# The order of work inside the chunk loop of a decoder layer: state product, right sides and first mask

## The chip, the cores and the metric

The kernel runs on one core of one Trainium2 chip. The metric is the device time of one execution in microseconds; of several executions the median counts. The profile is that of one execution, which has a time of its own.

## The reference

One layer of a hybrid decoder over 16 learned meta tokens and 2048 real tokens, width 1024. The input is RMS-normalised and projected once; then two branches read it. Branch B is stick-breaking attention and is not touched here. Branch A is RWKV-7 time mixing with 16 heads of dimension 64, whose core is a delta-rule recurrence over the tokens:

```
sa    = einsum("bhvk,bhk->bhv", state, kk)
state = state * decay - sa * (kk * a) + v * k
y     = einsum("bhvk,bhk->bhv", state, r)
```

After it each head's output is centred, divided by its standard deviation, and given a gain and a bonus. Both branches are gated, projected, merged and projected once more; the result is normalised and added to the input.

## The kernel before

The kernel has four stages one behind another: projections (up to about 2026 us), attention, the chunk loop of branch A (2956.7 to 3642.8 us of the span), and a tail with the branch and output projections. Only the chunk loop matters here; its functions are `tensor`, `scalar`, `vector`, `gpsimd` and `sync` inside `rwkv_programs`.

The recurrence is worked off in chunks of 64 tokens, 33 of them (`NCH`), padding and meta tokens in the first. Eight pairs of heads (`PAIRS`) lie on the 128 partitions, 64 for each head of a pair. For each chunk the kernel makes:

- **scores** (`score_products`, L1519): 16 matmuls of keys with queries into two double banks, `even` and `odd`. ScalarE copies one block of each to `NT` (L1660, L1661). VectorE masks all of it into `scores` (`masked`, L1717, two instructions);
- **the inverse of a triangular matrix** of 64x64 by blocks in five levels (`LEVELS`, `LAST` = 5). For each level `NT` is multiplied with that level's mask `tri` into `off` (L1767). A level is a `product` (L1582) of `off` with T, which VectorE makes into `X` (L1741), and an `advance` (L1595, in the last level L1597), which ScalarE copies to T or, in the last level, to `TT` (L1686), and VectorE transposes (L1751). Each is done in two halves of four pairs. T before level 1 is `off[0]` transposed (L1735), and the same with the unit matrix added (`tt_init`, L1785). Products and advances use the banks `even` and `odd` again;
- **right sides** (`right_sides`, L1552), which need the state before the chunk: ScalarE copies it beside the values (L1668, L1669, `s_kept`); then the **updates** `u` (L1560) with `TT`, copied by ScalarE (L1697, L1698); then the **state's product** (`next_state`, L1507) into the bank `chain`, to which VectorE adds the old state (L1727, `S_sum`) and which GpSimd scales (`S`, L1767, `s_done`);
- **outputs**: `value_products` (L1535) and `state_outputs` (L1568) into `y_bank`, centred values squared by ScalarE (L1674), the `variance` (L1527, L1528), the square root (L1702), reciprocals on VectorE (L1722) and three operations of GpSimd.
- **turned keys** (`turn_keys`, L1543), copied by ScalarE to `KBt` (L1653), for the state's product.

Every engine walks through bodies n = 0 to 36 (`walk`), and what follows the inverse lags: body n makes scores and inverse of chunk n, right sides, state outputs and updates of n - 1, and state's product and value products of n - 2. Each engine executes in the order written. TensorE's order in a body is state's product of n - 2, scores of n, value products of n - 2, key turns of n, right sides of n - 1, and then per level: product, something `beside_product`, advance, something `beside_advance`. What lies beside: state outputs in levels 1 and 2, updates in 3 and 4, the variance in 5. Order between engines is by semaphores that count up; `reach(eng, name, count)` waits for one. The scores of chunk n wait for all copies out of both banks of the chunk before:

```
reach(pe, "x_out", 10 * n)
reach(pe, "t_out", 10 * n)
```

All five masks of a chunk are made by GpSimd, and count on `off_done`. In the bodies 1 to 3 ScalarE and VectorE also split weights and outputs for the tail into high and low parts (L1706 to L1758).

Of the kernel before, what the change touches and what calls it, by code (L numbers as in the profile page):

```python
# [13 lines left out]
P = 128  # L14
# [1367 lines left out]
def rwkv_programs(nc, sem, t, io, scratch, tail, r, opening, y_parts_sent):  # L1382

    with ExitStack() as ctx:
# [11 lines left out]
        names = """zeroed kbt_pe kbt_out st_pe nt_out st_out off_done tt_init t0_out x_pe x_out t_pe t_out tt_out  # L1396
# [101 lines left out]
        def tensor(pe):  # L1498
# [74 lines left out]
            def body(n, b, turn):  # L1573
                def product(lv, half):
                    reach(pe, "off_done", LAST * n + lv)
# [24 lines left out]
                def beside_product(lv):  # L1600
# [9 lines left out]
                    if lv == 5 and inside(n, 2, 1):  # L1610
                        variance(n - 2, n)

# [11 lines left out]
                if inside(n, 2) and n <= NCH:  # L1624
                    next_state(n - 2)
                if inside(n, 0):
                    score_products(n, turn)
                if inside(n, 2, 1):
                    value_products(n - 2)
                if inside(n, 0):  # L1630
                    turn_keys(n)
                if inside(n, 1):
                    right_sides(n - 1)
# [14 lines left out]
        def scalar(act):  # L1648
# [6 lines left out]
            def body(n, b, turn):  # L1655
                b1, b2 = (b + 2) % 3, (b + 1) % 3
                if inside(n, 0):
                    reach(act, "st_pe", n + 1)
                    reach(act, "off_done", LAST * n)
                    act.copy(NT[0:DH, :, :], even[0:DH, :, 0:C]).then_inc(s["nt_out"], 1)  # L1660
                    act.copy(NT[DH:P, :, :], odd[DH:P, :, 0:C]).then_inc(s["nt_out"], 1)  # L1661
                if inside(n, 1):
                    reach(act, "s_done", n - 1)
                    if n == 1:
                        act.wait_ge(s["zeroed"], 1)
                    reach(act, "y_pe", n - 4)
                    reach(act, "s_pe", n - 3)
                    act.copy(VU[b1][0:DH, :, 0, :], S[b1][0:DH, :, :]).then_inc(s["s_kept"], 1)  # L1668
                    act.copy(VU[b1][DH:P, :, 1, :], S[b1][DH:P, :, :]).then_inc(s["s_kept"], 1)  # L1669
                if inside(n, 2, 1):  # L1670
# [41 lines left out]
        def vector(dve):  # L1712
            def body(n, b, turn):
# [10 lines left out]
                if inside(n, 2) and n <= NCH:  # L1724
                    reach(dve, "s_pe", n - 1)
                    reach(dve, "s_done", n - 2)
                    dve.tensor_tensor(S_sum[:, :, :], chain[:, :, :], S[b2][:, :, :], ALU.add).then_inc(s["s_sum"], 1)  # L1727
                if inside(n, 4, 1):
                    inverse_std(n - 4, slice(HP, PAIRS))
                if inside(n, 0):  # L1730
                    masked(0, even)
                    masked(1, odd)
                    for half in range(2):
                        reach(dve, "off_done", LAST * n + 1)
                        dve.transpose(T2[:, half, 0, :, :].rearrange("p k c -> p (k c)"),  # L1735
                                      off[0][:, HP * half:HP * half + HP, :].rearrange("p k c -> p (k c)")).then_inc(s["t0_out"], 1)
                for lv in range(1, LAST + 1):
# [5 lines left out]
                    if lv in (3, 4) and inside(n, 3, 1):  # L1743
                        inverse_std(n - 3, slice(lv - 3, lv - 2))
                    if lv == LAST and inside(n, 3, 1):
# [19 lines left out]
        def gpsimd(pool):  # L1765
# [3 lines left out]
            def body(n, b, turn):  # L1769
# [5 lines left out]
                if inside(n, 0):  # L1775
                    reach(pool, "nt_out", 2 * n + 2)
                    for lv in range(1, LAST + 1):
                        reach(pool, "x_pe", 10 * (n - 1) + 2 * lv)
                        if lv == 1:
                            reach(pool, "t0_out", 2 * n)  # L1780
                        tt(off[lv - 1][:, :, :], NT[:, :, :], tri[:, lv - 1, :].unsqueeze(1).broadcast_to(grid), ALU.mult, "off_done")
                        if lv == 1:
                            reach(pool, "t_pe", 10 * n)
                            reach(pool, "off_done", LAST * n + 1)
                            pool.tensor_tensor(T2[:, :, 1, :, :], off[0][:, :, :].rearrange("p (a k) c -> p a k c", a=2),  # L1785
                                               eye[:, :].unsqueeze(1).unsqueeze(1).broadcast_to([P, 2, HP, C]),
                                               ALU.add).then_inc(s["tt_init"], 1)
# [25 lines left out]
        def settled(eng):  # L1813

            banks_free(eng)
            for name, count in (("off_done", LAST * NCH), ("tt_init", NCH), ("t0_out", 2 * NCH), ("var_pe", NCH - 1), ("s_done", NCH - 1),
# [552 lines left out]
```

## Time and profile before

| | us |
|---|---|
| median of 3 runs | 4181.08 (4180.16 to 4187.48) |
| the profiled execution | 4177.68 |
| its span, first to last instruction | 4175.9 |
| the chunk loop in it | 2956.7 to 3642.8 |

| engine | busy share of the span | busy us in the chunk from 3250.40 to 3270.15 |
|---|---|---|
| TensorE (PE) | 97% | 19.20 of 19.75 |
| weight loads (PEld) | 80% | 17.84 |
| VectorE (DVE) | 56% | 14.63 |
| ScalarE (ACT) | 41% | 12.13 |
| GpSimd (POOL) | 20% | 13.53 |

Ends of matmuls are modelled, and the end of one overlaps the start of the next; so the length of a group of matmuls is best read from its start to the start of the next group.

### The profile page before, as it was taken

To read this page: it belongs to the slowest core of one execution; us is meant where nothing else is said; L and a number is where in the kernel's file an instruction comes from. 1 tells how busy PE (TensorE), PEld (TensorE's weight loads), DVE (VectorE), ACT (ScalarE), POOL (GpSimd) and SP (SyncE) were. 2 spreads that over 40 slices of the span, in tenths; PEclk is the share of its full clock that TensorE was granted. 3 is DMA by queue.
4 is the path that set the end of the run, shared out by engine and by line. 5 is a ranking of instruction groups with operands and counts; after the bars stand their busy time and mean duration, and the time that the engine had idled before them with its cause. 6 is when DMAs were issued, how large, how long until landed. Compare 5 with 4: busy or idle time off the path is not lost. (4 is left out here: it accounts for less than half of the span.)

```text
span 4175.9 us, 88867 instructions
## 1 busy us (share of the span) xinstructions
PE 4030.3 (97%) x34728; PEld 3322.7 (80%) x34728; DVE 2327.7 (56%) x3166; ACT 1709.1 (41%) x3428; POOL 817.4 (20%) x658
## 2 busy tenths in 40 slices
PE   7999999998899999999799999999899999999999
PEld 6888998887688888888566666666789988888887
DVE  5444545434643444444578888888567777633222
ACT  4222322222322222222376767676556665521111
POOL 3101111110211001111000000000256666600222
PEclk9999999999899999999899999999999999999999
DMA  2343333334233443433543344443333333265653
GB/s 90 116 124 116 111 109 94 109 116 149 66 109 114 121 121 114 121 102 116 132 98 85 83 94 100 96 101 67 100 112 107 106 108 115 80 218 166 208 176 126
DMA packets 482562, 479.67 MB, mean 115 GB/s; under 512 B 256784, under 2 KB 366992, under 8 KB 476128
## 3 DMA queue, kind: packets, MB, share of 16 engines
q1 hardware_dynamic: 469360, 445.85, 38.4%
q10 hardware_dynamic: 11520, 25.17, 1.7%
q0 software_dynamic: 1392, 4.54, 0.5%
q8 instruction: 212, 3.47, 0.3%
q14 instruction: 78, 0.64, 0.1%
HBM read 305.51 MB, written 169.93 MB: 114 GB/s over the span
## 5 line engine op out<-in xcount | busy, mean ns | idle before, releaser
L1251 ACT ACTIVATE keep<-z 128x512 f32<-128x512 f32 (+4 forms) x704 | 374.5, 539 | 192.7 <-PE z L1195 190.5
L1289 DVE TENSOR_TENSOR_SCAN kept<-keep,kept 128x512 f32<-128x512 f32 (+2 forms) x448 | 404.1, 954 | 26.7 <-ACT keep L1251 19.9
L1261 ACT COPY w<-turned 128x512 f32<-128x512 f32 (+4 forms) x704 | 371.5, 557 | 94.7 <-PE turned L1205 94.1
L1205 PE MATMUL turned<-t_identity,kept 128*128 128x128 f32 (+1 forms) x2432 | 364.2, 275 | 2.3 <-DVE kept L1289 2.3
L1286 DVE TENSOR_TENSOR_SCAN kept<-keep,hidden 128x512 f32<-128x512 f32 (+3 forms) x256 | 275.9, 1116 | 149.6 <-ACT keep L1251 148.9
L1194 PE MATMUL z<-k_high,q_parts 128*128 128x512 f32 (+4 forms) x704 | 303.3, 431 | 36.9 <-ACT keep L1251 16.7
L1205 PEld LDWEIGHTS turned<-t_identity,kept 128*128 128x128 f32 (+1 forms) x2432 | 280.2, 135 | 65.4 <-issue 12.4
L1232 PE MATMUL acc<-w,dv 128*64 128x512 f32 (+3 forms) x1280 | 288.1, 537 | 0.0
L1195 PE MATMUL z<-k_low,q_parts 128*128 128x512 f32 (+4 forms) x704 | 252.6, 359 | 0.0
L1767 POOL TENSOR_TENSOR off<-NT,tri 128x512 f32<-128x512 f32 x165 | 205.9, 1275 | 139.7 <-ACT NT L1661 139.7
L1194 PEld LDWEIGHTS z<-k_high,q_parts 128*128 128x128 f32 x704 | 133.8, 190 | 98.1 <-issue 42.8
L1232 PEld LDWEIGHTS acc<-w,dv 128*64 128x64 f32 x1280 | 94.4, 137 | 134.2 <-issue 120.8
L1582 PE MATMUL even<-T,off 64*64 64x64 f32 x5280 | 194.9, 222 | 4.3 <-issue 2.1
L1582 PEld LDWEIGHTS even<-T,off 64*64 64x64 f32 x5280 | 174.9, 136 | 18.2 <-issue 3.5
L1311 POOL DMA_DIRECT2D dv_diag<-scr_v_edge x15 | 7.3, 487 | 838.2 <-DMA dv_diag<-scr_dv 838.2
L1751 DVE STREAM_TRANSPOSE T<-T 128x256 f32<-128x256 f32 x264 | 117.6, 445 | 87.8 <-ACT T L1686 85.0
L1686 ACT COPY T<-odd 128x256 f32<-128x256 f32 x264 | 98.3, 373 | 158.7 <-PE odd L1595 146.9
L1741 DVE TENSOR_TENSOR X<-even,eye 128x256 f32<-128x256 f32 x330 | 139.4, 422 | 41.0 <-PE even L1582 33.5
L2108 DVE TENSOR_TENSOR y_lo<-y_raw,y_hi 128x512 fp32r<-128x512 f32 x61 | 44.8, 734 | 205.2 <-ACT y_hi L2052 205.2
L1595 PE MATMUL odd<-X,T 64*64 64x64 f32 x4224 | 151.8, 220 | 2.2 <-issue 1.8
L794 DVE CAST w_hi0B<-w_raw0B 128x1024 fp32r<-128x1024 f32 x40 | 41.7, 1042 | 197.6 <-PE pp3B L340 69.3
L794 DVE CAST w_hi0A<-w_raw0A 128x1024 fp32r<-128x1024 f32 x40 | 32.6, 815 | 203.0 <-PE pp4A L340 76.4
(566 smaller groups left out, 10880.7 us busy)
## 6 DMA issues: line engine op xcount, KB each, us to landing
w_raw0A<-in_w_main SPq DMA_DIRECT2D x42, 512.0 KB, 3.8
w_raw0B<-in_w_main SPq DMA_DIRECT2D x42, 512.0 KB, 3.8
w_raw1A<-in_w_main SPq DMA_DIRECT2D x41, 512.0 KB, 3.9
w_raw1B<-in_w_main SPq DMA_DIRECT2D x41, 512.0 KB, 3.9
KB<-scr_kb SPq DMA_DIRECT2D x33, 512.0 KB, 5.2
AR<-scr_ar SPq DMA_DIRECT2D x33, 512.0 KB, 5.9
y_raw<-scr_y SPq DMA_DIRECT2D x64, 256.0 KB, 4.4
merge<-scr_merge SPq DMA_DIRECT2D x64, 256.0 KB, 5.8
```

Of the source, the lines that this page charges most:

```text
L1194: pe.matmul(out, queries, k_high[u][:, k0:k0 + size], start=True, stop=False)
L1195: pe.matmul(out, queries, k_low[u][:, k0:k0 + size], start=False, stop=True).then_inc(logits_done, 1)
L1205: mm = pe.transpose(turned[num % TB][0:size, P * r:P * r + P], kept[kept_in(g)][:, src:src + size], t["identity"][:, :])
L1232: mm = pe.matmul(out, lhs, rhs, start=start, stop=stop, skip_group_check=True)
L1251: act.activation(keep[num % KB][:, 0:size], z[num % ZB][:, 0:size], ACT.Sigmoid, scale=-DH ** -0.5).then_inc(keep_done, 1)
L1261: act.copy(w[num % WB][0:size, c0:512], turned[num % TB][0:size, c0:512]).then_inc(copied, 1)
L1286: dve.tensor_tensor_scan(dst, data, hidden[:, 512 - size:][:, ::-1], 1.0, ALU.mult, ALU.max).then_inc(scanned, 1)
L1289: dve.tensor_tensor_scan(dst, data, data, kept[kept_in(g)][:, end:end + 1], ALU.mult, ALU.bypass).then_inc(scanned, 1)
L1582: mm = pe.matmul(x_bank(half)[hs, k, :], off[lv - 1][hs, HP * half + k, :], T2[hs, half, 0, k, :], start=True, stop=True)
L1595: mm = pe.matmul(p_bank(half)[hs, 0, k, :], T2[hs, half, 1, k, :], X[hs, half, k, :], start=True, stop=True)
L1741: dve.tensor_tensor(X[:, half, :, :], x_bank(half), eye[:, :].unsqueeze(1).broadcast_to([P, HP, C]), ALU.add).then_inc(s["x_out"], 1)
L1767: pool.tensor_tensor(out, a, b, op).then_inc(s[name], 1)
```

## The change

Three things move. On TensorE the state's product of chunk n - 1 stands in body n beside the fifth level's product, ahead of the advance, where before it was first in body n + 1; VectorE's sum moves with it. Right sides stand directly behind the scores; ScalarE makes its two copies of the state ahead of the two NT copies. And the first of the five masks is made by VectorE instead of GpSimd, between its two masked scores, with a semaphore of its own (`off_first`), on which the transposes and `tt_init` wait; `off_done` counts the other four.

```diff
@@ tensor
                 def product(lv, half):
-                    reach(pe, "off_done", LAST * n + lv)
+                    if lv > 1:
+                        reach(pe, "off_done", (LAST - 1) * n + lv - 1)
@@ beside_product
                     if lv == 5 and inside(n, 2, 1):
                         variance(n - 2, n)
+                    if lv == 5 and inside(n, 1) and n < NCH:
+                        next_state(n - 1)
@@ body
-                if inside(n, 2) and n <= NCH:
-                    next_state(n - 2)
                 if inside(n, 0):
                     score_products(n, turn)
+                if inside(n, 1):
+                    right_sides(n - 1)
                 if inside(n, 2, 1):
                     value_products(n - 2)
                 if inside(n, 0):
                     turn_keys(n)
-                if inside(n, 1):
-                    right_sides(n - 1)
@@ scalar
-                if inside(n, 0):
-                    reach(act, "st_pe", n + 1)
-                    reach(act, "off_done", LAST * n)
-                    act.copy(NT[0:DH, :, :], even[0:DH, :, 0:C]).then_inc(s["nt_out"], 1)
-                    act.copy(NT[DH:P, :, :], odd[DH:P, :, 0:C]).then_inc(s["nt_out"], 1)
...
                     act.copy(VU[b1][DH:P, :, 1, :], S[b1][DH:P, :, :]).then_inc(s["s_kept"], 1)
+                if inside(n, 0):
+                    reach(act, "st_pe", n + 1)
+                    reach(act, "off_done", (LAST - 1) * n)
+                    reach(act, "off_first", n)
+                    act.copy(NT[0:DH, :, :], even[0:DH, :, 0:C]).then_inc(s["nt_out"], 1)
+                    act.copy(NT[DH:P, :, :], odd[DH:P, :, 0:C]).then_inc(s["nt_out"], 1)
@@ vector
-                if inside(n, 2) and n <= NCH:
-                    reach(dve, "s_pe", n - 1)
-                    reach(dve, "s_done", n - 2)
-                    dve.tensor_tensor(S_sum[:, :, :], chain[:, :, :], S[b2][:, :, :], ALU.add).then_inc(s["s_sum"], 1)
...
                     masked(0, even)
-                    masked(1, odd)
+                    reach(dve, "nt_out", 2 * n + 2)
+                    reach(dve, "tt_init", n)
+                    reach(dve, "x_pe", 10 * n - 8)
+                    dve.tensor_tensor(off[0][:, :, :], NT[:, :, :], tri[:, 0, :].unsqueeze(1).broadcast_to(grid),
+                                      ALU.mult).then_inc(s["off_first"], 1)
                     for half in range(2):
-                        reach(dve, "off_done", LAST * n + 1)
+                        reach(dve, "off_first", n + 1)
                         dve.transpose(...).then_inc(s["t0_out"], 1)
+                    masked(1, odd)
...
+                    if lv == LAST and inside(n, 1) and n < NCH:
+                        reach(dve, "s_pe", n)
+                        reach(dve, "s_done", n - 1)
+                        dve.tensor_tensor(S_sum[:, :, :], chain[:, :, :], S[b1][:, :, :], ALU.add).then_inc(s["s_sum"], 1)
@@ gpsimd
-                    for lv in range(1, LAST + 1):
+                    reach(pool, "t_pe", 10 * n)
+                    reach(pool, "off_first", n + 1)
+                    pool.tensor_tensor(T2[:, :, 1, :, :], off[0]..., eye..., ALU.add).then_inc(s["tt_init"], 1)
+                    for lv in range(2, LAST + 1):
                         reach(pool, "x_pe", 10 * (n - 1) + 2 * lv)
-                        if lv == 1:
-                            reach(pool, "t0_out", 2 * n)
                         tt(off[lv - 1][:, :, :], NT[:, :, :], tri[:, lv - 1, :]..., ALU.mult, "off_done")
-                        if lv == 1:
-                            reach(pool, "t_pe", 10 * n)
-                            reach(pool, "off_done", LAST * n + 1)
-                            pool.tensor_tensor(T2[:, :, 1, :, :], off[0]..., eye..., ALU.add).then_inc(s["tt_init"], 1)
```

## Rows read from the trace of the kernel before

**Rows 1.** Busy time by stretch: window, length, PE, PEld, DVE, ACT, POOL, PEclk, DMA.
```profile
2981.80:3001.70 19.90, 17.15 (x458) 15.84 (x459) 13.39 (x27) 11.54 (x24) 8.55 (x8) 1.00 0.22 69
3250.40:3270.15 19.75, 19.20 (x522) 17.84 (x523) 14.63 (x29) 12.13 (x26) 13.53 (x11) 1.00 0.37 105
3069.83:3611.97 542.14, 523.34 (x14095) 485.01 (x14095) 396.39 (x757) 328.29 (x676) 365.17 (x297) 1.00 0.38 107
```
**Rows 2.** Waits from 3000 to 3600: waiter, releaser, us in total, times, longest.
```profile
PE chain L1552 <- ACT VU L1669: 22.0, 30, 3.2
```
**Rows 3.** Timeline ahead of the scores: start, us, engine, line, operation, [idle before].
```profile
3282.42 0.58 ACT L1698 COPY VU<-chain 64x512 f32<-64x512 f32 x1
...
3283.34 1.15 PE L1597 MATMUL odd<-T,X 64*64 64x64 f32 x32
...
3284.42 1.15 PE L1507 MATMUL chain<-VU,KBt 128*64 128x64 f32 x32
3284.93 0.69 ACT L1702 ACTIVATE rstd<-flip,t_eps 128x512 f32<-128x512 f32 x1
...
3285.50 0.37 PE L1519 MATMUL even<-AR,KB 64*128 64x128 f32 x1
...
3286.39 1.04 POOL L1767 TENSOR_TENSOR S<-S_sum,t_w_end 128x512 f32<-128x512 f32 x1 [4.80 <-DVE S_sum L1727]
```
**Rows 4.** Timeline of the same chunk behind the scores.
```profile
3287.48 1.15 PE L1535 MATMUL y_bank<-scores,VU 128*64 128x64 f32 x32
...
3288.21 1.22 DVE L1717 TENSOR_TENSOR scores<-even,full 128x1024 f32<-128x1024 f32 x1 [0.25 <-ACT NT L1660]
...
3288.57 1.09 PE L1543 MATMUL flip<-t_identity,KB 128*128 128x128 f32 x8
3288.81 0.62 ACT L1668 COPY VU<-S 64x512 f32<-64x512 f32 x1
...
3289.35 1.21 DVE L1717 TENSOR_TENSOR scores<-odd,full 128x1024 f32<-128x1024 f32 x1
3289.45 0.61 ACT L1669 COPY VU<-S 64x512 f32<-64x512 f32 x1
...
3290.21 1.15 PE L1552 MATMUL chain<-VU,scores 128*64 128x64 f32 x32 [0.56 <-ACT VU L1669]
3290.29 1.28 POOL L1785 TENSOR_TENSOR T<-off,eye 128x512 f32<-128x512 f32 x1
3290.48 0.76 DVE L1735 STREAM_TRANSPOSE T<-off 128x256 f32<-128x256 f32 x2
...
3291.29 1.15 PE L1582 MATMUL even<-T,off 64*64 64x64 f32 x32
...
3292.02 0.89 DVE L1741 TENSOR_TENSOR X<-even,eye 128x256 f32<-128x256 f32 x2 [0.78 <-PE even L1582]
...
3292.63 1.10 PE L1595 MATMUL odd<-X,T 64*64 64x64 f32 x32
```
**Rows 5.** Timeline between the chunks 0 and 1.
```profile
2975.33 1.18 PE L1597 MATMUL odd<-T,X 64*64 64x64 f32 x32
...
2976.06 0.87 ACT L1686 COPY TT<-odd 128x256 f32<-128x256 f32 x2 [1.57 <-PE odd L1597]
...
2977.08 0.34 PE L1519 MATMUL even<-AR,KB 64*128 64x128 f32 x1 [0.56 <-ACT TT L1686]
```
**Rows 6.** One line's instructions: duration in ns minimum/median/maximum, first and last start.
```profile
L1758 DVE TENSOR_TENSOR y_lo<-y_raw,y_hi x3: 684/685/686, 2997.8 to 3043.6; 128x512 fp32r<-128x512 f32 x3
```
**Rows 7.** Timeline: right sides made in the bodies 1, 2, 4 and 33.
```profile
2981.78 1.15 PE L1552 MATMUL chain<-VU,scores 128*64 128x64 f32 x32 [1.62 <-ACT VU L1669]
...
3001.67 1.69 PE L1552 MATMUL chain<-VU,scores 128*64 128x64 f32 x32 [2.42 <-ACT VU L1669]
...
3047.48 1.97 PE L1552 MATMUL chain<-VU,scores 128*64 128x64 f32 x32 [3.20 <-ACT VU L1669]
...
3630.39 1.98 PE L1552 MATMUL chain<-VU,scores 128*64 128x64 f32 x32 [2.36 <-ACT VU L1669]
```

More of the change, by code:

```diff
@@ L1394, in rwkv_programs @@
         y_bank = ctx.enter_context(nc.psum_tensor("y_bank", grid, F32))
-        names = """zeroed kbt_pe kbt_out st_pe nt_out st_out off_done tt_init t0_out x_pe x_out t_pe t_out tt_out
+        names = """zeroed kbt_pe kbt_out st_pe nt_out st_out off_first off_done tt_init t0_out x_pe x_out t_pe t_out tt_out
             r_pe r_out u_pe u_even u_odd s_pe s_sum s_done s_kept ar_kept ys_pe y_pe yc_out sq_out sq_high sq_low var_pe std_done rstd_done
@@ L1776, in body @@
                     reach(pool, "nt_out", 2 * n + 2)
-                    for lv in range(1, LAST + 1):
+                    reach(pool, "t_pe", 10 * n)
+                    reach(pool, "off_first", n + 1)
+                    pool.tensor_tensor(T2[:, :, 1, :, :], off[0][:, :, :].rearrange("p (a k) c -> p a k c", a=2),
+                                       eye[:, :].unsqueeze(1).unsqueeze(1).broadcast_to([P, 2, HP, C]),
+                                       ALU.add).then_inc(s["tt_init"], 1)
+                    for lv in range(2, LAST + 1):
                         reach(pool, "x_pe", 10 * (n - 1) + 2 * lv)
-                        if lv == 1:
-                            reach(pool, "t0_out", 2 * n)
                         tt(off[lv - 1][:, :, :], NT[:, :, :], tri[:, lv - 1, :].unsqueeze(1).broadcast_to(grid), ALU.mult, "off_done")
-                        if lv == 1:
-                            reach(pool, "t_pe", 10 * n)
-                            reach(pool, "off_done", LAST * n + 1)
-                            pool.tensor_tensor(T2[:, :, 1, :, :], off[0][:, :, :].rearrange("p (a k) c -> p a k c", a=2),
-                                               eye[:, :].unsqueeze(1).unsqueeze(1).broadcast_to([P, 2, HP, C]),
-                                               ALU.add).then_inc(s["tt_init"], 1)
                 if inside(n, 2, 1):
@@ L1815, in settled @@
             banks_free(eng)
-            for name, count in (("off_done", LAST * NCH), ("tt_init", NCH), ("t0_out", 2 * NCH), ("var_pe", NCH - 1), ("s_done", NCH - 1),
+            for name, count in (("off_first", NCH), ("off_done", (LAST - 1) * NCH), ("tt_init", NCH), ("t0_out", 2 * NCH), ("var_pe", NCH - 1), ("s_done", NCH - 1),
                                 ("rstd_done", 5 * (NCH - 1)), ("y_done", NCH - 1)):
```

## Prediction

> **What bounds the kernel now.** I read the share of busy time first, then the stretch of the chunk loop, then one chunk in order of time. TensorE is busy 97% of the span, so the question is where it is not. The change touches only the chunk loop, from 2956.7 to 3642.8 us. A chunk in the middle of it lasts 19.75 us, of which TensorE works 19.20 at a granted clock of 1.00 [rows 1]. The table of waits over thirty chunks has one wait of TensorE that matters: the right sides wait for ScalarE's copy of the state, 30 times, 22.0 us together [rows 2]. In the timeline of one chunk that wait is the 0.56 us ahead of the right sides (L1552). Ends overlap the next start, so I count from start to start: the eight key turns begin at 3288.57, and eight at the pace of their weight loads (some 0.11 us each) need 0.93, so the right sides could begin at 3289.50; they begin at 3290.21 [rows 4]. The true hole is 0.71 us.
>
> Why it is there: the state's product is issued last in front of the scores (3284.42), GpSimd's scaling of the state's sum begins at 3286.39, and ScalarE can take the copies only after both NT copies, at 3288.81 and 3289.45 [rows 3, 4]. All else in the chunk is TensorE behind TensorE. So in this loop time is won only by closing that hole, and lost by every wait put elsewhere on TensorE.
>
> I name two instants, with which all that follows is counted. **A** is the start of the fifth level's advance (L1597), **Q** is the start of the first group behind the scores (3287.48, there L1535).
>
> **Part 1: the state's product goes ahead of the fifth level's advance.** TensorE's work is the same: both groups take 1.08 from start to start (3283.34, 3284.42, 3285.50) [rows 3]. The product needs ScalarE's two copies of u; the second ends at 3283.00 (3282.42 + 0.58), and the product's new place is at 3283.34, so it does not wait in the middle of the loop [rows 3]. The start-up chunks have no variance ahead of it and may wait 0.1 to 0.4 there. The state is ready 1.08 earlier.
>
> What was covered by it is uncovered. The scores write both banks from which ScalarE copies the last T (t_out 10n, L1515). Before, the state's product ran for 1.08 between the advance and the scores, and the copies hid under it. Now nothing stands between. The trace holds one instance of exactly this, since chunk 0 has no state's product behind it: advance at 2975.33, both copies from 2976.06 to 2976.93, first score at 2977.08, marked as a wait for the TT copy [rows 5]. That is 1.75 from start to start where 1.08 is free, so 0.67; in that instance the advance itself was 0.03 longer. Worked out from its pieces: 1.15 for the advance, 0.42 until the second copy's end (2976.93 against 2976.51), 0.15 to TensorE's start, is 1.72, and a few hundredths of it are the longer advance. I take 1.70, **a new hole of 0.62 us per chunk**, with bounds of 0.55 and 0.67. Scores now begin at A + 1.70.
>
> **Part 2: right sides directly behind the scores, ScalarE's state copies ahead of its NT copies.** The state: its product begins at A - 1.08; GpSimd's scaling begins 1.97 after the product and takes 1.04 (3284.42, 3286.39) [rows 3], so S is there at A + 1.95. ScalarE is done with TT at A + 1.55, then has the square root (0.69 long, its successor 0.6 to 0.7 behind) [rows 3], and is free at A + 2.2. Its two copies start 0.64 apart and take 0.62 (3288.81, 3289.45), and TensorE starts 0.14 behind (3290.21 against 3290.07) [rows 4]: right sides possible at A + 3.60. The scores last 1.98 (3285.50 to 3287.48) [rows 3, 4], so Q is A + 3.68. The old hole of 0.71 closes, with 0.08 to spare, and ScalarE is free for the NT copies at the moment the scores end. The margin is thin, but a miss of 0.1 costs nothing, as part 3 shows. In VectorE's order the state sum moves to level 5, ahead of two reciprocals; it now waits there for the product, but the 1.74 reciprocal behind it still ends 1 us ahead of the NT copy. Loads from memory keep their places: SyncE's program is not changed.
>
> **Part 3: who lets level 1 begin.** TensorE alone would need 1.08 (right sides), 1.09 (value products), 0.93 (key turns) and 1.34 (first product and state outputs, 3291.29 to 3292.63) until the advance of level 1: Q + 4.44 [rows 4]. Before it was at Q + 5.15. So 0.71 would be won if nothing else came late. But VectorE does. The first masked scores begin at Q + 0.73 (3288.21). Then, in VectorE's order:
> - masked scores of the even bank, start to start 1.14 (3288.21, 3289.35) [rows 4];
> - the first mask, new on VectorE. No row shows it; the nearest is a two-input operation on the same 128x512 float32 in SBUF, 0.685 [rows 6]. Bounds: 0.60, that row less the overlap with a successor, and 1.28, GpSimd's own time for such a tile (3290.29) [rows 4]. I take 0.69, since engine, size and operands are those of rows 6, and 0.05 for the wait on its own result;
> - two transposes, together 0.76 [rows 4], of which 0.70 to the successor's start;
> - masked scores of the odd bank, moved behind the transposes, 1.14;
> - the first X, 0.43 (half of 0.89 less the wait between), and 0.05 to TensorE [rows 4].
>
> The transposes are ready at Q + 0.73 + 1.88 + 0.42, which is Q + 3.03, in time for the first product at Q + 3.10. That is what the mask's move gives. But X comes at 0.73 + 1.14 + 0.74 + 0.70 + 1.14 + 0.43 + 0.05, so the advance can't begin before **Q + 4.95**. Before the change both masked scores were done by 3290.56 and X followed the product at once (3292.02) [rows 4]. So 0.20 of the 0.71 is won; 0.51 stays as a wait of the advance for X. The bounds of this term are 0.12 and 0.30 won. If right sides or NT copies came 0.1 late, TensorE would still wait for X. GpSimd's masks of the later levels start with the T init at Q + 2.64 instead of Q + 2.81 [rows 4], so none is late. GpSimd loses 1.28 us of work per chunk, which it has to spare.
>
> What a page says on moving the mask: the Trainium skill, GPSIMD Engine Reference, section 4.1 (Engine selection), gives elementwise work on a tile to VectorE, GpSimd being about twice as slow with two inputs; the rows agree for the operation itself (1.28 against 0.685). By that rule alone the mask leaves the path to the first product and the whole 0.71 is won; by the order on VectorE only 0.20 is. I count by the order, and the rule is the first rival below.
>
> **The sum.** Per chunk 0.62 - 0.20 = **0.42 us lost**. It holds for the chunks whose predecessor and self are in steady state, n = 5 to 32, 28 of them: 11.8 us.
>
> Start of the loop, n = 2 to 4: here ScalarE and VectorE split tail weights between the chunks, and the right sides wait 2.42 and 3.20 us, each followed by matmuls at half pace (32 in 1.69 and 1.97 where 1.15 is usual) [rows 7]. The state's sum no longer stands behind VectorE's splits, but ScalarE's casts still stand ahead of its state copies, and now ahead of the NT copies too, and only 1.98 us of TensorE work covers them instead of about 4. Followed chunk by chunk I get 0.9 won at n = 2, 0.3 lost at n = 3, and at n = 4 0.4 won or 1.7, as the clock falls or not: 1 us won, bounds 4 won and 1 lost.
>
> End of the loop, n = 33: no scores cover the state copies, and the value products now stand behind the right sides, which wait 2.4 us and run at half pace as they do now (2.36 and 1.98) [rows 7]. The last outputs' squares, which need these products, the R copy behind them on ScalarE and the last updates come later, by 1.9; bounds 0 and 3. The tail's first matmuls wait for the loop's last banks, so this passes through.
>
> Sum: 11.8 - 1 + 1.9 = 12.7 us. The profiled execution took 4177.68 us (span 4175.9), which gives 4190.4; the median of the runs is 4181.08, 3.4 above it, which gives 4193.8. I predict the middle, 4192.
>
> **Rivals.**
> - *The mask's move frees the whole path (the page's rule).* If VectorE gets through its chain by Q + 4.4, the advance is bound by TensorE. Then 0.62 - 0.71 is 0.09 won per chunk, 2.5 in 28, and with -1 and +1.9 the time is 1.6 below: 4179 by the median. Against it: the sum of five rows on one in-order engine. It would need 0.5 us less out of 4.2.
> - *Not slower: the scores are not held by the TT copies.* If in the loop TensorE began the scores within 0.1 of the advance's end, only the 0.20 won is left, 5.6 us in 28, some 5 below before: 4176. It decides at a hole of 0.20 per chunk, under which the change wins. Against it is the one instance [rows 5], whose wait is explicit.
> - *Stalls in TensorE's instruction supply fall into the new waits.* From the right sides that start at 3069.83 to those at 3611.97 lie 27 chunks in 542.14 us, 20.08 each, against some 19.8 of an undisturbed one [rows 1]. If the two new waits took up these 8 us of stray stalls, the loss would be about 5: 4186.
> - *The clock falls in each chunk.* Two holes lie within 6 us of each other now. After waits of 2.42 and 3.20 the matmuls run at half pace for several us [rows 7], which cost some 1.5 us at n = 2. In 28 chunks that is 42 us more: 4235. Against it: the right sides at 2981.78 come after a wait of 1.62 and run at full pace, and their chunk is at 1.00 [rows 1, 7], and the new holes are 0.62 and 0.51. The Trainium skill, TensorE: Matmul & The Clock Gate, section "HAM oscillation — how this bites in real kernels", tells that idle gaps in each turn of a loop can bring the lower of the two levels (1.2 and 2.4 GHz) back every turn; the trace shows this only behind the long waits.
>
> **How the numbers follow.** Forecast 0.65, mask rival 0.12, scores not held 0.05, stalls taken up 0.12, clock 0.06. The measurement tells some 0.2% (8.4 us) from no change. The forecast's own range from its bounds: per chunk 0.25 to 0.55, so 7 to 15 us, with start and end 3 to 19: 4184 to 4200. Of its 0.65 I count 0.05 below 8.4 and none faster. Faster gets a part of the two winning rivals with a better start than thought, 0.06; same 0.28; slower 0.66. The range for 8 in 10 goes from 4180, which takes in the stalls and most of the mask rival, to 4202.
>
> **What would show it.** In the profile after: waits of the scores (L1519's new line) for TT some 31 times at 0.4 to 0.6; no wait of the right sides in the middle of the loop; a wait of level 1's advance for X of 0.3 to 0.5; chunks of about 20.2 us. Wrong if the first X begins before Q + 4.0, if scores start less than 1.3 behind the advance, or if the granted clock of middle chunks is under 1.00.

## The result

The changed kernel takes 4198.34 us, the median of six runs (4191.66 to 4201.23), against 4180.90 for the kernel before (4179.93 to 4187.48): 17.4 us slower, ratio 1.0039 with a 95% interval of 1.0029 to 1.0049. The forecast was slower, 4192, with a range to 4202. All medians here and below leave out the few executions of 4383 us and more, which ran in a slower state of the chip.

The busy shares of the page barely move: TensorE from 97% to 96% of the span, VectorE 56% as before, GpSimd from 20% to 18%. The waits of the stretch from 3000 to 3600 us show what changed. Columns: waiter, releaser, us in total, times, longest.

```profile
ACT TT L1688 <- PE odd L1598: 62.2, 28, 3.3
...
PE even L1519 <- ACT TT L1688: 15.8, 28, 0.6
...
PE even L1583 <- issue: 6.5, 13, 0.9
...
PE chain L1552 <- ACT VU L1665: 3.9, 3, 2.6
...
PE odd L1596 <- DVE X L1744: 3.3, 19, 0.2
```

The wait of the right sides [rows 2] is down to the start-up chunks. Each chunk now waits ahead of its scores, for the copy of TT. And TensorE's gaps marked issue, in which no other engine is named, have grown: ahead of products alone to 6.5 us from 2.1, over all its lines to 14.6 from 4.3.

One chunk of the changed kernel in order of time, to be held against rows 3 and 4 (start, us, engine, line, operation, idle before):

```profile
3251.02 1.15 PE L1507 MATMUL chain<-VU,KBt 128*64 128x64 f32 x32
3252.10 1.15 PE L1598 MATMUL odd<-T,X 64*64 64x64 f32 x32
...
3254.91 0.62 ACT L1665 COPY VU<-S 64x512 f32<-64x512 f32 x1
3255.80 1.15 PE L1552 MATMUL chain<-VU,scores 128*64 128x64 f32 x32
...
3256.52 1.22 DVE L1719 TENSOR_TENSOR scores<-even,full 128x1024 f32<-128x1024 f32 x1 [1.12 <-ACT NT L1670]
3256.78 1.10 PE L1535 MATMUL y_bank<-scores,VU 128*64 128x64 f32 x32
3257.66 0.68 DVE L1733 TENSOR_TENSOR off<-NT,tri 128x512 f32<-128x512 f32 x1
3257.82 1.09 PE L1543 MATMUL flip<-t_identity,KB 128*128 128x128 f32 x8
...
3258.37 0.77 DVE L1737 STREAM_TRANSPOSE T<-off 128x256 f32<-128x256 f32 x2
...
3258.97 1.15 PE L1583 MATMUL even<-T,off 64*64 64x64 f32 x32
3259.07 1.19 DVE L1719 TENSOR_TENSOR scores<-odd,full 128x1024 f32<-128x1024 f32 x1
...
3260.18 0.74 DVE L1744 TENSOR_TENSOR X<-even,eye 128x256 f32<-128x256 f32 x2
3260.64 1.15 PE L1596 MATMUL odd<-X,T 64*64 64x64 f32 x32 [0.18 <-DVE X L1744]
```

With A = 3252.10 and Q = 3255.80 the right sides start directly behind the scores, ScalarE's state copy having ended at 3255.53. The advance of level 1 starts at Q + 4.84 (5.15 before). VectorE goes from masked scores to mask, transposes, masked scores and X without a pause, and TensorE waits for X. In the next chunk, A is 3272.36 and the first score 3274.07, 1.71 behind it:

```profile
3272.36 1.15 PE L1598 MATMUL odd<-T,X 64*64 64x64 f32 x32
...
3273.09 0.84 ACT L1688 COPY TT<-odd 128x256 f32<-128x256 f32 x2 [2.15 <-PE odd L1598]
...
3274.07 0.34 PE L1519 MATMUL even<-AR,KB 64*128 64x128 f32 x1 [0.56 <-ACT TT L1688]
```

**Where the time went.** A chunk in which nothing odd happens now lasts 20.16 us (from right sides to right sides, 3317.63 to 3337.79) where it lasted 19.78 (3250.37 to 3270.15). The 28 steady chunks, from the fifth level's last advance of chunk 4 to that of chunk 32, first before and then changed:

```profile
3062.95:3624.87 561.92, 542.56 (x14618) 502.88 (x14617) 411.05 (x785) 340.44 (x700) 378.70 (x308) 1.00 0.38 107
```
```profile
3063.07:3647.59 584.52, 548.95 (x14620) 505.47 (x14616) 423.92 (x812) 338.04 (x700) 342.58 (x280) 1.00 0.36 103
```

(Columns as in rows 1.) The spans differ by 23.2 us, more than the medians. The loop's first score starts 1.9 later (2956.70 and 2958.55), which is the stages ahead of it and none of the change; the start of the loop up to chunk 4 is 2.8 shorter, the 28 chunks are 22.6 longer, and what follows is 1.6 longer. (The 28 chunks are cut at the fifth level's advance, ahead of which the state's product now stands; its 1.08 us are counted with what follows, as before.) Of the 22.6, 28 times 0.38 is 10.6. The other 12.0 are **stray time**, by which I mean what the chunks take beyond 28 undisturbed ones: 561.92 - 553.8 = 8.1 us before, 584.52 - 564.5 = 20.0 now. It shows mostly as breaks inside groups of matmuls for which no other engine is named, such as this one:

```profile
3284.66 0.33 PE L1583 MATMUL even<-T,off 64*64 64x64 f32 x4
3285.33 1.03 PE L1583 MATMUL even<-T,off 64*64 64x64 f32 x28 [0.34 <-issue]
```

The experiments have two tasks: to confirm the two waits that make the 0.38, and to find out where the stray time comes from.

### The profile page after: what moved, and what is told of

It is laid out like the page before. It is cut to its first block and busy times, and to the rows that moved or that the text cites. A ratio compares the mean times of both kernels' runs of the same rounds, so it can differ in the third digit from the quotient of the medians.

```text
span 4199.1 us, 88867 instructions
## 1 busy us (share of the span) xinstructions
PE 4035.7 (96%) x34728; PEld 3322.4 (79%) x34728; DVE 2343.2 (56%) x3199; ACT 1706.0 (41%) x3428; POOL 774.6 (18%) x625
## 5 line engine op out<-in xcount | busy, mean ns | idle before, releaser
L1774 POOL TENSOR_TENSOR off<-NT,tri 128x512 f32<-128x512 f32 x132 | 163.7, 1273 | 0.0
L1596 PEld LDWEIGHTS odd<-X,T 64*64 64x64 f32 x4224 | 140.0, 136 | 12.4 <-DVE X L1744 8.7
```

Of the source, the lines that this page charges most:

```text
L1596: mm = pe.matmul(p_bank(half)[hs, 0, k, :], T2[hs, half, 1, k, :], X[hs, half, k, :], start=True, stop=True)
L1774: pool.tensor_tensor(out, a, b, op).then_inc(s[name], 1)
```

## The experiments

Each kernel was timed beside the kernel before on the same chip, whose median there was 4181.67 (state's product alone to half of the masked scores), 4181.01 (both with fewer loads, the kernel before shifted, the state copy) and 4181.38 (the changed kernel shifted, the cover, the repeats). Ratios are to that kernel. The changed kernel's 4198.34 is from the first comparison. "Undisturbed" is the commonest shortest chunk, read as above; stray time is counted over the 28 chunks of one profile.

### The state's product alone

```diff
 kernel before, body of TensorE
-                if inside(n, 2) and n <= NCH:
-                    next_state(n - 2)
 beside_product, level 5, behind the variance
+                    if lv == 5 and inside(n, 1) and n < NCH:
+                        next_state(n - 1)
 (VectorE's S_sum moves to level 5 as in the change)
```

> The kernel before with the state's product (and VectorE's sum) ahead of the fifth advance, all else as before. Theory (the product was the cover of the TT copies): the scores begin 1.71 us behind the advance instead of 1.08 us behind it with the state's product between, so 0.62 is lost per chunk; the right sides still wait, since ScalarE makes its state copies behind the NT copies, so the hole of 0.7 ahead of them stays. Undisturbed chunk 19.78 + 0.62 = 20.40 us, in 28 chunks 17 us, total +17 to +25 with whatever instruction stalls come on top. Rival (the state comes earlier, so the right sides do too): right sides' wait shrinks by what is lost, undisturbed chunk 19.8, total within 3 us of before. Second question: TensorE's gaps marked as issue from chunk 5 on are 3.6 us in the kernel before and 16.2 us in the changed one; if the wait ahead of the scores brings them, they are 10 us or more here, if the early right sides or the mask bring them, 3 to 5.

Measured: 4201.57 us (ratio 1.0048, 1.0031 to 1.0065), undisturbed chunk 20.40, stray time 15.4. Both waits stand side by side in TensorE's waits from 3070 to 3612 (in the same stretch of the kernel before the right sides wait 28 times for 15.6 us):

```profile
PE even L1519 <- ACT TT L1686: 14.7, 26, 0.6
PE chain L1552 <- ACT VU L1669: 13.6, 25, 0.5
```

The undisturbed chunk is 0.62 longer to the hundredth, and the right sides wait nearly as before. The removed cover costs 0.62 with the right sides in their old place too. On the stray time it gave no clean answer: 15.4 lies between the first profiles of the two kernels, and so do the issue gaps, some 7 us where 10 or more, or 3 to 5, were expected.

### The mask back on GpSimd

```diff
 changed kernel, VectorE (GpSimd makes off[0] and counts it on off_done, as before)
                     masked(0, even)
+                    masked(1, odd)
-                    dve.tensor_tensor(off[0]..., NT..., tri...).then_inc(s["off_first"], 1)
                     for half in range(2):
                         dve.transpose(...)
-                    masked(1, odd)
```

> The changed kernel with the first mask back on GpSimd (both masked scores first on VectorE, then the transposes). Theory (VectorE's queue, masked scores of the odd bank ahead of X, binds the first advance at Q + 4.84 to 4.89): with GpSimd's mask the transposes are ready at about Q + 3.45, the first product starts there, and the first advance at Q + 4.8, so the undisturbed chunk is 20.1 us, within 0.1 of the changed kernel's 20.16: the mask's move is worth nothing. Rival (the mask on VectorE brings the gain): without it the first product is 0.6 later and the undisturbed chunk is 20.6 to 20.8, total 15 us above the changed kernel. Issue gaps: if the mask's move brought them, 3 to 5 us, else 10 to 18.

Measured: 4199.87 us (1.0041, 1.0027 to 1.0056), undisturbed chunk 20.16, stray time 25.1. The chunk is the same to the hundredth with and without the mask's move. What binds has changed place only: the first product now waits for the transposes, 22 times for 10.2 us, and X is there when its time comes.

```profile
PE even L1582 <- DVE T L1731: 10.2, 22, 0.5
```

The mask's move is worth nothing in this order of work, and it isn't what brings this kernel's stray time either. Part of the 25.1 is the clock: twice in these chunks a break is followed by matmuls at half pace, as here.

```profile
3531.68 0.84 PE L1543 MATMUL flip<-t_identity,KB 128*128 128x128 f32 x4 [2.55 <-issue]
3532.45 1.98 PE L1582 MATMUL even<-T,off 64*64 64x64 f32 x32
```

### The mask alone

```diff
 kernel before, with the changes of the mask only:
 off[0] by VectorE between masked(0, even) and masked(1, odd), off_first
```

> The kernel before with the first mask on VectorE alone. Theory: the right sides still wait for ScalarE's state copies until Q + 2.7, so the first product cannot begin before Q + 3.8, and X is there by then; undisturbed chunk 19.78 within 0.1, total within 4 us of before. Rival (VectorE's queue binds even here, since masked scores of the odd bank stand ahead of X): first advance at Q + 5.3 or later, undisturbed chunk 19.9 to 20.1, total +5 to +10.

Measured: 4186.46 us (1.0011, 1.0001 to 1.0021), undisturbed chunk 19.78, stray time 16.3. From 3070 to 3612 the right sides wait 26 times for 14.5 us (15.6 before). The chunk did not move, as the theory said; the total went up by 4.8 all the same, a little beyond the 4 that it gave. TensorE's instructions and their order are those of the kernel before, but for one semaphore for which the first product no longer waits. So an edit that leaves TensorE's work and its undisturbed chunk alone seems to cost stray time; the lower end of the interval is close to no change.

### Half of the masked scores left out

```diff
 changed kernel, masked()
+                    kn = HP if h and n >= 3 else PAIRS
+                    ks = slice(0, kn)
-                    dve.tensor_tensor(scores[h][b][:, :, :], src[:, :, :],
+                    dve.tensor_tensor(scores[h][b][:, ks, :], src[:, ks, :],
```

> The changed kernel with the masked scores of the odd bank for only four of the eight pairs from chunk 3 on; the other four keep what an earlier chunk left (that part of the computation is left out). It takes some 0.53 us from VectorE's queue between the transposes and X and changes nothing else. Theory (VectorE's queue binds the first advance): the advance comes at Q + 4.5 instead of Q + 4.87, the undisturbed chunk is 19.75 to 19.85, some 10 us in all below the changed kernel. Rival (TensorE binds the first advance, VectorE has slack): no difference from 20.16.

Measured: 4192.07 us (1.0029, 1.0015 to 1.0043), undisturbed chunk 19.76, stray time 19.6. VectorE and TensorE behind scores that end with Q = 3209.36:

```profile
3212.64 0.65 DVE L1721 TENSOR_TENSOR scores<-odd,full 128x512 f32<-128x512 f32 x1
3213.25 0.89 DVE L1746 TENSOR_TENSOR X<-even,eye 128x256 f32<-128x256 f32 x2
```
```profile
3209.36 1.15 PE L1552 MATMUL chain<-VU,scores 128*64 128x64 f32 x32
...
3213.84 1.13 PE L1596 MATMUL odd<-X,T 64*64 64x64 f32 x32
```

With 0.53 us less in VectorE's queue, the first advance starts at Q + 4.48 instead of Q + 4.84, which is TensorE's own limit (Q + 4.44 by rows 4). VectorE's queue was the bound. The total fell by 6.3 of the 10 expected. The undisturbed chunk is that of the kernel before or shorter, and yet the kernel is 10.4 us slower than it. That made the stray time the main question.

### Fewer loads

```diff
 both kernels, SyncE
-                    load_keys(n + 1, nb)
+                    if n < 2:
+                        load_keys(n + 1, nb)
+                    else:
+                        sp.sem_inc(kb_in[nb], 16)
 (load_queries in the same way with ar_in)
```

> The changed kernel with keys and queries loaded for the first three chunks only (the later ones compute on stale ones: 1 MB of transfers per chunk left out, nothing else). In the changed kernel's profile chunks that nothing disturbs last 20.16 us, and the mean of the 28 steady ones is 20.88: 0.72 of stray time per chunk, which falls inside groups of matmuls as gaps marked issue. Theory (instructions for TensorE arrive late, because their transfers share the DMA engines with the loads): with half of the traffic gone the mean chunk is 20.2 to 20.35 and the total 12 to 18 us below the changed kernel. Rival (the stray time has nothing to do with the loads): the mean chunk stays 20.7 to 21.0.

> The same on the kernel before: keys and queries loaded for three chunks only (computes on stale ones after that). Undisturbed chunks last 19.78 us, the mean of the steady ones is 20.07, 0.29 stray. Theory (late instructions by shared DMA engines): mean chunk 19.8 to 19.9, total 6 to 8 us below before; the difference to the same edit on the changed kernel is then that of the undisturbed chunks, 0.38 each, 11 us, and 13 in all with start and end. Rival: mean chunk stays at 20.0 to 20.1, and the difference between the two edited kernels is 17 as between the unedited.

Measured: the changed kernel with fewer loads takes 4187.14 us (1.0014, 1.0004 to 1.0024), the kernel before with fewer loads 4178.45 (0.9993, 0.9983 to 1.0002). The 28 chunks of the first, and of the second:

```profile
3060.98:3631.84 570.86, 546.44 (x14621) 503.69 (x14618) 423.10 (x812) 337.89 (x700) 342.55 (x280) 1.00 0.22 56
```
```profile
3058.96:3623.43 564.47, 543.74 (x14617) 503.56 (x14616) 411.06 (x785) 340.20 (x700) 378.23 (x308) 1.00 0.23 57
```

The DMA engines' share falls from 0.36 and 0.38 to 0.22 and 0.23. In the changed kernel the stray time falls from 20.0 to 6.4 us and the total by 11.2. In the kernel before it does not fall (10.6 in this profile, 8.1 with all loads); the total is 2.6 lower. Undisturbed chunks stay at 20.16 and 19.78. The two edited kernels differ by 8.7 us, where the unedited ones differ by 17. So about half of the slowdown is extra stray time that exists only beside the loads of keys and queries. The rest of the stray time, 6 to 11 us, is in every kernel and doesn't come from these loads; that half of the expectation was wrong.

### Instructions shifted

```diff
 both kernels, TensorE, ahead of the chunk loop
+            for _ in range(128):
+                pe.sem_inc(shift, 1)
```

> The kernel before with 127 further instructions in TensorE's program ahead of the chunk loop, each adding to a semaphore nobody waits for (some microseconds at the loop's start while TensorE would wait anyway for loads, at most 4 us by themselves); the loop's own order is not touched, only where its instructions lie in the program. Theory (how much stray time falls into the loop depends on where blocks of instructions end against the loads, and the kernel before happens to lie well): undisturbed chunk 19.78 as before, but the mean rises from 20.07 to 20.3 to 20.7, total +5 to +17. Rival (stray time comes from the order of work that was changed): mean 20.0 to 20.15, total +0 to +4.

> The changed kernel with the same 127 further instructions in TensorE's program ahead of the loop as in the shifted kernel before, where they cost 17 us by the fifth chunk and raised the stray time of the 28 steady chunks from 8 to 12 us. Theory (stray time depends on where blocks of instructions end against the loads): undisturbed chunk 20.16, stray time of the 28 chunks moves by 5 us or more from its 20, more likely down, so that the total is 4205 to 4213. Rival (the stray time belongs to the changed order): it stays at 18 to 22, total 4214 to 4217.

Measured: before, shifted, 4202.20 us (1.0047, 1.0031 to 1.0064); changed, shifted, 4213.82 (1.0079, 1.0061 to 1.0097). The loop adds 128 increments (the expectations say 127), and they are dear. The last advance of chunk 4 starts at 3080.27 instead of 3062.95, 17.3 later; I had allowed 4. Less that, the shifted kernel before is 3.9 us slower than the unshifted, with an undisturbed chunk of 19.78 and 12.1 us of stray time, 4.0 more. The shifted changed kernel is 1.8 us faster than the unshifted changed one after the same deduction; that is its time alone, no stray time was read for it, and the time lies between what the theory and the rival gave. The deduction itself is good to 2 us only: in a second profile of the unshifted kernel before, below, that advance is at 3064.60 and the stray time 11.1. So where the instructions lie moves the stray time by some 4 us at most, hardly more than two executions differ. It does not explain the 20, which fits the rival: the extra belongs to the order of work.

### The state copy on GpSimd, a candidate

```diff
 kernel before, GpSimd, behind S (ScalarE keeps the even copy in body 1 only)
+                    tt(VU[(b + 2) % 3][0:DH, :, 0, :], S_sum[0:DH, :, :], t["w_end"]..., ALU.mult, "s_kept")
```

> A candidate, on the kernel before: from chunk 1 on GpSimd writes the even heads' state into the operand of the right sides itself (the same product once more on 64 partitions, behind the state), so that ScalarE makes only the odd copy behind its NT copies. By the kernel before's rows ScalarE's copy then ends at Q + 1.95 instead of Q + 2.58, TensorE could begin the right sides at Q + 2.1 where it is free at Q + 2.02, and the first product is then held by VectorE's transposes at about Q + 3.45. Theory: undisturbed chunk 19.78 - 0.34 = 19.4 to 19.5 us, 10 us less in the loop. Rival (GpSimd's extra operation delays the first mask, or the copy of ScalarE was not what the right sides wait for): undisturbed chunk 19.7 or more.

Measured: 4179.05 us (0.9990, 0.9980 to 1.0000), undisturbed chunk 19.54, stray time 18.7. The old hole does close, and the first product waits for the transposes instead, 25 times for 8.2 us:

```profile
PE even L1582 <- DVE T L1736: 8.2, 25, 0.3
```

I had expected 19.4 to 19.5. The gain of 0.24 per chunk, 6.7 in 28, reaches the total as 2.0; the profile has more stray time than either of the kernel before. It is the fastest kernel of the study that computes the whole layer, by an amount that the interval hardly tells from nothing.

### The cover put back

```diff
 changed kernel, TensorE
-                if inside(n, 2, 1):
-                    value_products(n - 2)
 beside_advance
+                    if lv == 5 and inside(n, 1, 1):
+                        value_products(n - 1)
```

> The changed kernel with the value products of chunk n - 1 behind the fifth advance of body n, where they cover the TT copies, instead of between right sides and key turns a body later. Theory (new hole is the missing cover; the first advance is held by VectorE at Q + 4.87 whatever TensorE does): the scores no longer wait for TT, but begin 2.16 us behind the advance, the first product waits for the transposes for another microsecond, and the first advance stays at Q + 4.8 to 4.9: undisturbed chunk 20.16 + 0.45 = 20.6 us, total +12 on the changed kernel. Rival (TensorE's own work sets the first advance): Q + 3.9 to 4.0, undisturbed chunk 19.6, total 15 below the changed kernel.

Measured: 4202.24 us (1.0050, 1.0032 to 1.0068), undisturbed chunk 20.62, stray time 14.6. One chunk on TensorE:

```profile
3207.23 1.15 PE L1598 MATMUL odd<-T,X 64*64 64x64 f32 x32
3208.30 1.15 PE L1535 MATMUL y_bank<-scores,VU 128*64 128x64 f32 x32
3209.39 0.37 PE L1519 MATMUL even<-AR,KB 64*128 64x128 f32 x1
...
3211.37 1.15 PE L1552 MATMUL chain<-VU,scores 128*64 128x64 f32 x32
3212.45 1.09 PE L1543 MATMUL flip<-t_identity,KB 128*128 128x128 f32 x8
3214.55 1.15 PE L1583 MATMUL even<-T,off 64*64 64x64 f32 x32 [1.00 <-DVE T L1737]
...
3216.22 1.15 PE L1596 MATMUL odd<-X,T 64*64 64x64 f32 x32 [0.18 <-DVE X L1744]
```

With work between the advance and the scores, the wait for TT is gone, so it was a matter of cover and nothing else. But the first advance stays at Q + 4.85, although TensorE has a microsecond less to do before it: from the scores to the first advance this loop runs at VectorE's pace. Moving TensorE's work out of that stretch wins nothing and costs its own length elsewhere. The total rose by 3.9 on the changed kernel and not by the 12 expected; less stray time accounts for 5.4 of the difference by the changed kernel's first profile and for 0.8 by its second, below.

### Both kernels once more

> The changed kernel once more, for a second profile: undisturbed chunk 20.16 again; stray time of the 28 steady chunks 20 us in the first profile, 15 to 25 here if it is a property of the kernel, and anywhere from 5 to 25 if it is one of the execution.

> The kernel before once more, for a second profile: undisturbed chunk 19.78 again; stray time of the 28 steady chunks 8 us in the first profile, 5 to 12 here if it is a property of the kernel, up to 25 if it is one of the execution.

Measured, one execution each: 4195.60 us for the changed kernel and 4182.04 for the one before. The 28 chunks, changed and then before:

```profile
3061.41:3641.37 579.96, 548.36 (x14620) 505.21 (x14617) 423.91 (x812) 338.19 (x700) 342.50 (x280) 1.00 0.37 104
```
```profile
3064.60:3629.57 564.97, 544.16 (x14617) 503.65 (x14616) 411.21 (x785) 340.41 (x700) 378.40 (x308) 1.00 0.38 107
```

Undisturbed chunks are 20.16 and 19.78 again; they are exact from one execution to the next. Stray time is not: 15.5 and 11.1 us here against 20.0 and 8.1 in the first pair. The executions of one kernel scatter by 3 to 5 us in it, so a single profile cannot rank kernels by stray time, but the kernel before is the lower one both times. In this pair the spans differ by 13.5: the first score 1.8 earlier, the loop's start 2.5 shorter, the 28 chunks 15.0 longer, what follows 2.8 longer.

**What the stray time is.** The traces settle it. Count all of TensorE's records from the span's start, weight loads, matmuls and semaphore waits, and take every place inside a group of matmuls in the 28 chunks at which a weight load starts over 0.3 us behind the one before. In the thirteen profiles used here (all but that of the changed kernel shifted) there are 234 such places, and all of them lie a multiple of 256 records apart, to within one; in the shifted kernel before, with its 128 increments counted. The same traces show DMA packets of a kind called instruction, one for each 256 records:

```profile
q8 instruction: 117, 1.92, 1.3%
```

(28 chunks of the changed kernel: packets, MB, share.) At each of the 234 places the last of these packets, 16384 bytes, landed 1.2 to 2.0 us before TensorE went on. So a break is TensorE waiting for its next block of instructions. The 28 chunks are 30072 records in both kernels, some 117 blocks, of which 28 and 22 come visibly late in the changed kernel's two profiles (21 and 15 us together), 11 and 16 in the kernel before's (6 and 8 us), 8 and 14 with fewer loads. Some are late by the same amount in both kernels, such as this one, first before and then changed:

```profile
3543.19 0.45 PE L1582 MATMUL even<-T,off 64*64 64x64 f32 x8 [0.89 <-issue]
```
```profile
3563.91 0.45 PE L1583 MATMUL even<-T,off 64*64 64x64 f32 x8 [0.89 <-issue]
```

The packets themselves are hardly slower at the breaks (median 1.05 us for 0.96 at the other blocks, changed kernel); what is late is their start, a median 2.2 us after TensorE went over to the block before, where it is otherwise 1.5.

## Why the prediction was right, and where it was wrong

- **The new hole ahead of the scores: right.** 1.70 from advance to scores was predicted, 1.71 is in the timeline, and the kernel with the state's product alone loses 0.62 per chunk. One row between chunks 0 and 1 [rows 5] carried the whole term.
- **The old hole closes, with a thin margin: right.** Q is A + 3.70 (predicted 3.68), and ScalarE's state copy ends 0.27 ahead of the right sides. (Its rows put the state's arrival at A + 1.93, not A + 1.95; nothing hangs on it.)
- **VectorE binds the first advance: right in mechanism, 0.11 too late in size.** Q + 4.95 was predicted and Q + 4.84 came, so 0.31 of the 0.71 was won and not 0.20. Of the 0.11, 0.02 is a slip of addition: the terms as listed give Q + 4.93. The overlaps of VectorE's successive instructions make 0.06: from its first masked scores (3256.52) to X (3260.18) it takes 3.66 where I had summed 3.72. The remaining 0.03 lies in the first masked scores' start (Q + 0.72 for 0.73) and in X with its hand-over (0.46 for 0.48). The mask was 0.68 (predicted 0.69). Half of the masked scores left out shows the bound directly, and the cover put back shows it from the other side.
- **The net per chunk: 0.38 instead of 0.42.** The two terms give 0.31 (0.62 less 0.31). Of the remaining 0.07, 0.05 lies behind the first advance, where TensorE takes 0.98 from advance to state outputs (3260.64 to 3261.62) for 0.93. It belongs to the wait for X: in undisturbed chunks it is 0.98 here and with the cover put back, where the advance waits for X, and 0.93 with the mask on GpSimd and with half of the masked scores, where X is there. The other 0.01 to 0.02 is the new hole, 0.63 by the starts of its groups.
- **The start and the end: right in direction, within their bounds.** The start was to win 1 and won 2.8 and 2.5 in the two pairs; the end was to lose 1.9 and lost 1.6 and 2.8. The half pace that the prediction expected of the last right sides came in one of the changed kernel's profiles and not in the other.
- **Wrong: stray time was taken as unchanged, and its rival had the wrong sign.** I had let it be taken up by the new waits. It grew by 12.0 us in the profile of the result and by 4.3 in the second pair. The prediction's own terms with their measured sizes, as means of the two pairs, are 10.6 - 2.7 + 2.2 = 10.1, against 12.7 forecast and 17.4 measured; the missing 7 us are stray time, which had no term in the sum. That the time still lies within the range is luck: the range was wide for other reasons. With half of the loads gone the changed kernel loses 13.6 us of stray time by the first profile (9.1 by the second), and the difference of the two kernels is 8.7 us, near the 10.1.
- **The mask rival fell**, and with it the page's rule as a forecast of time. By the Trainium skill, GPSIMD Engine Reference, section 4.1, the operation belongs to VectorE, and it is indeed shorter there (0.68 for 1.28). The changed kernel without the move has the same chunk of 20.16.
- **The clock rival fell.** The granted clock is 1.00 over the 28 chunks of every kernel whose row is shown above. The new waits of 0.6 and 0.4 us in each chunk didn't bring the lower level. The Trainium skill, TensorE: Matmul & The Clock Gate, section "HAM oscillation — how this bites in real kernels", tells how waits in each turn of a loop can bring it back every turn; these did not. Stray breaks brought it in two kernels: half pace followed breaks of 1.45 and 2.55 us with the mask on GpSimd (0.99 over its 28 chunks) and one of 1.58 us with half of the masked scores, but not one of 2.33 us in the changed kernel. So the prediction's argument that a wait of 1.62 had left the pace full does not carry far.

**What stays open:** why the kernel before has so little stray time beside the same loads. That the extra is bound to the loads is shown for the changed kernel, and that stray time is late blocks of instructions is shown by the places of the breaks. The state's product alone, the mask alone and the order without the mask each had more of it in one profile (15.4, 16.3 and 25.1 us, for 8.1 and 11.1 in the kernel before), the first two by little more than two executions of one kernel differ. What makes a block's transfer start late, and which meeting of a load with TensorE's progress does it, was not isolated.

## What to carry to other kernels

Before an operation is moved, ask what it covers where it stands: here 1.08 us of matmuls hid a copy that the next group waits for, and the one place in the trace where the cover was already missing gave the price to the hundredth. Then follow each engine's own queue across the stretch; the first advance was VectorE's, so taking a wait away from TensorE, or a mask from GpSimd, moved the wait and not the time. And compare two kernels by their undisturbed chunk first and by their total second: a gain of a few tenths of a microsecond per turn of a loop can be eaten by stray time that no engine's queue explains. Where a break stands inside a group of equal instructions, count the engine's records between breaks: a fixed step means that the engine waited for its own instructions.

## What was not expected of the hardware

- An undisturbed chunk repeats to 0.01 us, while the stray time of the same program varies between 15.5 and 20.0 us, and 8.1 and 11.1, in two executions each.
- TensorE's breaks come at every 256th of its records or not at all (234 of 234), and a break inside a group can bring the lower clock level (2.55 us, then 32 matmuls in 1.98 us for 1.15).
- 128 semaphore increments on TensorE ahead of the loop start 0.16 us apart (2958.01 to 2978.05). The loop's first score is 21.6 us later for them, chunk 4's last advance 17.3.
- The same wait at the same place brings the lower clock level in one execution and not in the next. In the last body the right sides of the changed kernel come after a wait of 2.42 us and run at full pace in its first profile, at half pace in its second; those of the kernel before, after 2.36 us, at half pace in the first [rows 7] and at full pace in the second.

```profile
3651.16 1.15 PE L1552 MATMUL chain<-VU,scores 128*64 128x64 f32 x32 [2.42 <-ACT VU L1665]
```
```profile
3644.94 1.97 PE L1552 MATMUL chain<-VU,scores 128*64 128x64 f32 x32 [2.42 <-ACT VU L1665]
```
```profile
3635.10 1.15 PE L1552 MATMUL chain<-VU,scores 128*64 128x64 f32 x32 [2.36 <-ACT VU L1669]
```

(Changed kernel, its first and second profile; kernel before, its second.)
